# Decode attention in a hybrid encoder step: one sequence and four feature tiles at a time, instead of four sequences and one tile

## What is computed

```python
# fox: 8 heads of 64; diff: 4 heads, two maps of 64 each, values of 128
s = einsum('bqhd,bkhd->bhqk', q, concat(past_k, k)) * SCALE
s = s + cum[q] - cum[k]              # fox, and causal
s = s + bias[t5_bucket(k - q)]       # diff
p = softmax(s, axis=-1)
o = einsum('bhqk,bkhd->bqhd', p, concat(past_v, v))
# diff: a = p[map 0] - lam * p[map 1], then the same product
```

## Time and profile before

| | us |
|---|---|
| median of 3 runs | 2665.81 |
| lowest, highest | 2657.16, 2668.44 |
| profiled execution, its own time | 2663.46 |
| its span in the profile | 2661.7 |
| TensorE busy | 2517.9 (95%) |
| weight loads on TensorE busy | 2015.3 (76%) |
| VectorE busy | 1392.0 (52%) |
| ScalarE busy | 939.1 (35%) |
| GpSimd busy | 390.5 (15%) |
| granted TensorE clock, mean of the span | 0.978 |

### The profile page before, as it was taken

The page is one execution under the profiler, slowest core; times in us unless marked ns, Lnnn a source line. Parts: engine busy times, 40 slices in busy tenths (PEclk is TensorE's granted clock), DMA queues, the critical chain, the costliest instruction groups (busy, mean ns, idle before and its releaser), DMA issues.

```text
span 2661.7 us, 35813 instructions
## 1 busy us (share of the span) xinstructions
PE 2517.9 (95%) x13841; PEld 2015.3 (76%) x13841; DVE 1392.0 (52%) x2235; ACT 939.1 (35%) x1837; POOL 390.5 (15%) x398
## 2 busy tenths in 40 slices
PE   7999999998899999989989899899989989999998
PEld 5788888888799899989975565565556556888897
DVE  4311124413443333443248788788778876655553
ACT  4123331111122222100116655664664666422221
POOL 1100001131100000012244103213211340100000
PEclk9999999999899999999989999899999999999999
DMA  4543335448889889875842235055052322544432
GB/s 133 158 125 112 109 101 146 137 133 193 220 208 207 191 201 217 214 181 159 220 132 63 52 77 127 5 128 123 9 124 56 81 68 85 182 143 139 133 124 90
DMA packets 479945, 353.07 MB, mean 133 GB/s; under 512 B 189248, under 2 KB 443144, under 8 KB 473592
## 3 DMA queue, kind: packets, MB, share of 16 engines
q1 hardware_dynamic: 470640, 332.16, 48.8%
q0 software_dynamic: 9136, 18.63, 2.1%
HBM read 250.23 MB, written 100.19 MB: 132 GB/s over the span
## 4 chain that ended last, share of the span: by engine, by line
PE 73%; SPq 7%; DVE 6%; ACT 5%; issue 4%; DMA 4%; POOL 1%; DVEq 0%; ACTq 0%; POOLq 0%
PE p_acc L847 12%; PE p_acc L852 12%; PE p_acc L851 12%; PE a_op L2087 5%; PE a_sb L2062 4%; PE a_sb L2063 3%; PE a_op L2084 3%; SPq L467 3%; PE a_sa L2040 3%; PE a_sa L2043 2%; PE e_U L1404 2%; PE e_U L1405 2%; PE e_U L1406 2%; PE a_sa L2041 2%; ACT a_e L1900 2%
## 5 line engine op out<-in xcount | busy, mean ns | idle before, releaser
L847 PE MATMUL p_acc<-p_h_hi,p_w_hi 128*128 128x384 f32 (+1 forms) x1960 | 721.0, 368 | 9.4 <-DVE p_ev L559 8.0
L852 PE MATMUL p_acc<-p_h_hi,p_w_lo 128*128 128x384 f32 (+1 forms) x1920 | 689.2, 359 | 0.0
L851 PE MATMUL p_acc<-p_h_lo,p_w_hi 128*128 128x384 f32 (+1 forms) x1920 | 688.9, 359 | 0.0
L1931 DVE TENSOR_REDUCE a_nmax<-a_sa 128x1 f32<-128x1024 f32 (+7 forms) x384 | 347.2, 911 | 129.0 <-PE a_sa L2045 42.4
L1900 ACT ACTIVATE a_e<-a_sb 128x512 f32<-128x512 f32 (+3 forms) x640 | 310.4, 533 | 282.2 <-PE a_sb L2063 185.9
L847 PEld LDWEIGHTS p_acc<-p_h_hi,p_w_hi 128*128 128x128 f32 x1960 | 372.0, 190 | 48.2 <-DVE p_ev L559 8.3
L852 PEld LDWEIGHTS p_acc<-p_h_hi,p_w_lo 128*128 128x128 f32 x1920 | 362.9, 189 | 30.8
L851 PEld LDWEIGHTS p_acc<-p_h_lo,p_w_hi 128*128 128x128 f32 x1920 | 363.7, 189 | 28.7
L2062 PE MATMUL a_sb<-a_q,a_k 128*128 128x512 f32 (+2 forms) x640 | 277.3, 437 | 20.7 <-ACT a_e L1900 18.1
L661 DVE TENSOR_TENSOR p_w_lo<-p_raw,p_w_hi 128x1024 fp32r<-128x1024 f32 x96 | 129.5, 1349 | 304.5 <-ACT p_w_hi L592 304.5
L2063 PE MATMUL a_sb<-a_q,a_k 68*128 68x512 f32 (+2 forms) x640 | 237.9, 375 | 0.0
(11 more groups left out here) (228 smaller groups left out, 3569.4 us busy)
## 6 DMA issues: line engine op xcount, KB each, us to landing
p_raw<-in_w_in SPq DMA_DIRECT2D x98, 512.0 KB, 5.8
s_k_raw<-in_cache_fox_k SPq DMA_DIRECT2D x128, 128.0 KB, 3.8
s_v_raw<-in_cache_fox_v SPq DMA_DIRECT2D x32, 512.0 KB, 7.1
s_k_raw<-in_cache_diff_k SPq DMA_DIRECT2D x128, 128.0 KB, 3.9
s_v_raw<-in_cache_diff_v SPq DMA_DIRECT2D x32, 512.0 KB, 6.7
a_q<-scratch_q_hi SPq DMA_DIRECT2D x32, 512.0 KB, 13.3
a_k<-scratch_k_hi SPq DMA_DIRECT2D x32, 512.0 KB, 15.4
e_pair<-scratch_gT SPq DMA_DIRECT2D x80, 192.0 KB, 2.7
```

The lines of the kernel that those rows point to most:

```text
L847: nc.tensor.matmul(acc[a % 2][:, 0:n], hi, h_hi[p][:, k, at:at + n], start=(k == 0), stop=False)
L851: nc.tensor.matmul(acc[a % 2][:, 0:n], hi, h_lo[p][:, k, at:at + n], start=False, stop=False)
L852: last = nc.tensor.matmul(acc[a % 2][:, 0:n], lo, h_hi[p][:, k, at:at + n], start=False, stop=(k == DK - 1))
L1931: nc.vector.tensor_reduce(nmax[:, b % 2, c, col:col + 1], scores_of(ev[1]), axes, ALU.max, negate=True).then_inc(a_maxed, 1)
```

## The change

A unit now takes one sequence and four feature tiles, all fox or all diff: unit n is sequence n % 8 and tiles 0 to 3 (n < 8) or 4 to 7. Units 0 to 7 are still the fox ones, and the slots of all events are the same.

- A past key row is loaded whole, 2048 bytes, in 8 loads of 128 rows (L466 of the new file) instead of 16 loads in pieces of 256 bytes. Past values come in one load of 2 MB in pieces of 2048 bytes, instead of four of 512 KB in pieces of 512.
- Partitions 32i to 32i + 31 of the turned keys now hold the i-th quarter of the keys, for 32 of the features of every tile. The scores are 4 x 4 x 4 = 64 matmuls of 32 partitions by 32 columns with 256 keys, and 16 for the new keys. `tab` is four banks, a quarter of the keys in each, 272 columns (256 and room for the 16 new ones, filled with -1e30 in the first three).
- The small loads become 16 of q, 4 of new keys, and of `add` 16 for a fox unit (its 16 last columns apart) or 8 for a diff one.
- `turn` has two banks in place of three, for every user: `H`, `T`, `F` and `E`.
- The output store of a unit goes to four tiles, in pieces of 64 bytes.

```diff
-        k_raw = r_.sb("k_raw", [P, SEQS, 2 * KT, 2, 32])
-        v_raw = r_.sb("v_raw", [P, SEQS, KT, P])
-        kT = r_.sb("kT", [P, SEQS, 2, PAST // 2])
+        k_raw = r_.sb("k_raw", [P, KT, WIDTH])
+        v_raw = r_.sb("v_raw", [P, KT, WIDTH])
+        kT = r_.sb("kT", [P, KT, 4 * FTS, 32])
...
-        tab = s.ps("tab", [P, 3 * 512])
-        turn = [s.ps(f"turn{i}", [P, 512]) for i in range(3)]
+        tab = s.ps("tab", [P, 4, 512])
+        turn = [s.ps(f"turn{i}", [P, 512]) for i in range(2)]
...
-        return n // 2, n % 2, n // 2 >= 4
+        return n % DEC_BATCH, n // DEC_BATCH * FTS, n >= DEC_BATCH
...
-                for b in range(SEQS):
+                keys = cache("k", n).rearrange("(q t r) n -> t q r n", q=4, r=32)
+                for t in range(KT):
                     if n:
-                        sp.wait_ge(k_turned, 2 * (SEQS * (n - 1) + b + 1))
-                    for h in range(2):
-                        for m in range(2):
-                            at = 64 * h + 32 * m
-                            sp.dma_start(k_raw[at:at + 32, b], keys_of(n, b, h, m)).then_inc(k_in[b], 16)
+                        sp.wait_ge(k_turned, KT * (n - 1) + t + 1)
+                    sp.dma_start(k_raw[:, t], keys[t]).then_inc(k_in[t // 2], 16)
...
+                for j in range(4):
+                    rows_j = slice(32 * j, 32 * j + 32)
+                    for i in range(4):
+                        sp.dma_start(q_bd[32 * i:32 * i + 32, j, :, j // 2, :],
+                                     d["qT"][ft:ft + FTS, rows_j, tok].rearrange("f p t -> p f t")).then_inc(small_in, 16)
+                    sp.dma_start(kT_new[P - 32:P, j], d["kT"][ft:ft + FTS, rows_j, tok].rearrange("f p t -> p f t")).then_inc(small_in, 16)
...
+                            sp.dma_start(add[r:r + DEC_SEQ, :, 0:QK], d["nckS"][row:row + 1, 0:PAST].to_broadcast([DEC_SEQ, PAST])
+                                         .rearrange("p (q n) -> p q n", q=4)).then_inc(small_in, 16)
+                            sp.dma_start(add[r:r + DEC_SEQ, 3, QK:QW], d["nckS"][row:row + 1, PAST:KEYS]
+                                         .to_broadcast([DEC_SEQ, DEC_SEQ])).then_inc(small_in, 16)
...
-                for b in range(SEQS):
-                    sp.dma_start(v_raw[:, b], cache("v", n, b).rearrange("(t p) n -> p t n", p=P)).then_inc(v_in, 16)
+                sp.dma_start(v_raw[:], cache("v", n).rearrange("(t p) n -> p t n", p=P)).then_inc(v_in, 16)
...
             n = turn_at[ev_]
-            if n >= 3:
-                pe.wait_ge(turn_taken, n - 2)
-            return turn[n % 3]
+            if n >= 2:
+                pe.wait_ge(turn_taken, n - 1)
+            return turn[n % 2]
...
-                for j in range(2):
-                    for h in range(2):
-                        half = slice(64 * h, 64 * h + 64)
-                        for b in range(SEQS):
-                            q = q_bd[half, j, b].rearrange("p m t -> p (m t)")
-                            nc.tensor.matmul(tab[b * 32:b * 32 + 32, h * 512:h * 512 + 512], q, kT[half, b, j, :],
-                                             start=(j == 0), stop=(j == 1))
+                for j in range(4):
+                    for i in range(4):
+                        part = slice(32 * i, 32 * i + 32)
+                        for f in range(FTS):
+                            q = q_bd[part, j, f].rearrange("p m t -> p (m t)")
+                            nc.tensor.matmul(tab[f * 32:f * 32 + 32, i, 0:QK], q, kT[part, :, 4 * f + j, :],
+                                             start=(j == 0), stop=(j == 3))
```

More of the change, by code:

```diff
@@ L307, in project, with small_total, cache @@
     last_chunk = lambda g: (g, len(chunks(g)) - 1)
-    OP = 1152
+    scores = tab[:, :, 0:QW]
+    o_sum, o_turned = tab[:, 0, 288:288 + P], tab[:, 1, 288:288 + HD]
     PASS0 = max(acc_at[a] for a in acc_at if a[0] < NT) + 1
-    S_SMALL, S_V, S_K = 16 * 18, 16 * 5, 16 * 4
+    S_V, S_K = 16 * 2, 16 * 2
     def unit(n):
-        return n // 2, n % 2, n // 2 >= 4
-    def cache(name, n, b):
-        ft, g, diff = unit(n)
-        src = d[("cache_diff_" if diff else "cache_fox_") + name][0]
-        src = src.rearrange("b n h m e -> b n (h m e)" if diff and name == "k" else "b n h e -> b n (h e)")
-        return src[g * SEQS + b][:, ft % 4 * P:ft % 4 * P + P]
-    def keys_of(n, b, h, m):
-        half = cache("k", n, b)[h * 512:(h + 1) * 512, m * HD:(m + 1) * HD]
-        return half.rearrange("(t p) (j c) -> p t j c", p=32, c=32)
+        return n % DEC_BATCH, n // DEC_BATCH * FTS, n >= DEC_BATCH
+    def small_total(n):
+        return 16 * sum(20 + (8 if unit(i)[2] else 16) for i in range(n + 1))
+    def cache(name, n):
+        b, _, diff = unit(n)
+        src = d[("cache_diff_" if diff else "cache_fox_") + name][0]
+        return src.rearrange("b n h m e -> b n (h m e)" if diff and name == "k" else "b n h e -> b n (h e)")[b]
     def x_rows(t):
@@ L449, in sync @@
                 n = ev_[1]
-                ft, g, diff = unit(n)
+                b, ft, diff = unit(n)
                 if n == 0:
@@ L641, in scalar @@
                     act.wait_ge(v_inverted, n)
-                nc.scalar.activation(e_s[:], tab[:, 0:KEYS], ACT.Exp, bias=s_stat[:, 0:1], accum_out=s_stat[:, 1:2]).then_inc(weighed, 1)
+                nc.scalar.activation(e_s[:], scores, ACT.Exp, bias=s_stat[:, 0:1], accum_out=s_stat[:, 1:2]).then_inc(weighed, 1)
             elif what == "C1":
                 act.wait_ge(past_turned, 2)
-                nc.scalar.copy(line[:, 0:PAST], tab[0:BH, 0:PAST]).then_inc(line_made, 1)
+                nc.scalar.copy(line[:, 0:PAST].rearrange("p (h n) -> p h n", h=2), tab[0:BH, 0:2, :]).then_inc(line_made, 1)
     def vector(dve):
@@ L768, in vector @@
                 diff = unit(n)[2]
-                dve.wait_ge(small_in, S_SMALL * (n + 1))
+                dve.wait_ge(small_in, small_total(n))
                 if not diff:
-                    tail = add[:, PAST:KEYS]
+                    tail = add[:, 3, QK:QW]
                     nc.vector.tensor_tensor(tail, tail, causal, ALU.add).then_inc(added, 1)
@@ L774, in vector @@
                 dve.wait_ge(scored, n + 1)
-                cut = tab[:, PAST - P:KEYS] if diff else tab[:, 0:KEYS]
-                term = add[:, 0:P + DEC_SEQ] if diff else add[:]
+                cut = tab[:, 3, QW - P - DEC_SEQ:QW] if diff else scores
+                term = add[:, 3, QW - P - DEC_SEQ:QW] if diff else add[:]
                 nc.vector.tensor_tensor(cut, cut, term, ALU.add).then_inc(added, 1)
                 dve.wait_ge(added, n + 1 + min(n + 1, 8))
-                nc.vector.tensor_reduce(s_stat[:, 0:1], tab[:, 0:KEYS], AX.X, ALU.max, negate=True).then_inc(maxed, 1)
+                nc.vector.tensor_reduce(s_stat[:, 0:1], scores, AX.XY, ALU.max, negate=True).then_inc(maxed, 1)
             elif what == "E":
@@ L796, in vector @@
                     dve.wait_ge(merged, n)
-                nc.vector.tensor_scalar(o_rows[:], tab[:, OP:OP + P], s_stat[:, 2:3], coef[:, 6:7] if diff else coef[:, 7:8],
+                nc.vector.tensor_scalar(o_rows[:], o_sum, s_stat[:, 2:3], coef[:, 6:7] if diff else coef[:, 7:8],
                                         ALU.mult, ALU.mult).then_inc(rows_made, 1)
@@ L913, in tensor @@
                 for kt in range(KT + 1):
-                    for b in range(SEQS):
-                        v = v_raw[:, b, kt, :] if kt < KT else v_new[:, b, :]
-                        last = nc.tensor.matmul(tab[b * 32:b * 32 + 32, OP:OP + P], eT[:, kt, b * 32:b * 32 + 32], v,
+                    for f in range(FTS):
+                        v = (v_raw[:, kt] if kt < KT else v_new)[:, f * P:(f + 1) * P]
+                        last = nc.tensor.matmul(o_sum[f * 32:f * 32 + 32], eT[:, kt, f * 32:f * 32 + 32], v,
                                                 start=(kt == 0), stop=(kt == KT))
@@ L922, in tensor @@
                 if unit(n)[2]:
-                    last = nc.tensor.matmul(tab[:, OP + P:OP + P + HD], o_rows[:], sel[:, 2 * HD:3 * HD], start=True, stop=True)
+                    last = nc.tensor.matmul(o_turned, o_rows[:], sel[:, 2 * HD:3 * HD], start=True, stop=True)
                 else:
                     for m in range(2):
-                        last = nc.tensor.matmul(tab[m * HD:(m + 1) * HD, OP + P:OP + P + HD], o_rows[:, m * HD:(m + 1) * HD],
+                        last = nc.tensor.matmul(o_turned[m * HD:(m + 1) * HD], o_rows[:, m * HD:(m + 1) * HD],
                                                 sel[:, m * HD:(m + 1) * HD], start=True, stop=True)
```

115 lines of the change are left out of this document (57 added, 58 removed).

## The result

| | before | after |
|---|---|---|
| median, us | 2661.86 (4 runs) | 2857.93 (4 runs) |
| lowest, highest | 2657.16, 2668.44 | 2854.84, 2859.99 |
| span of the profiled execution | 2661.7 | 2854.6 |

The ratio is 1.0734, 95% interval 1.0704 to 1.0764: the change makes the kernel 196 us slower. The forecast was 2651, the range ended at 2690, and the dearest rival stood at 2689. The sign was that of R3, the size and the reason were nobody's.

A forecast was written before the change was run, and what follows sets the result against it. It took the 600 to 1240 us stage as TensorE-bound with 31.8 us of holes: 2663.5 - 19 (holes, clock) + 2.4 (scores) + 3 + 1.5 (turn banks) = 2651.4, forecast 2651; own range 2643 to 2658, overall low 2625, high 2690.

The forecast's parts named there:

- R3: Rival, scores on TensorE: a pass costs 28 ns whichever tile, decisive from 15 ns; slower, 2689 us; chance 0.18.
- Eight key loads of 128 pieces then cost 8 x 0.57 = 4.6 us.: SyncE's queue, per unit: key loads at an unhindered issue's price take 4.6 us instead of 12.1.
- A fox burst is then 4.6 + 8.6 + 7.3 = 20.5 us against 20.5 now: no gain.: SyncE's issue of one fox unit's keys, q with new keys, and add rows: 20.5 us, as long as before.
- "(b)" to "(e)": TensorE holes going: before o_rows, all 8.6 us; before unit 2's scores, 3.5; diff units, all 7.1; short ones, all 1.0.
- The value load, 0.6 us.: SyncE's queue: one value load costs 0.6 us if room counts pieces, gaining 6.4 us a unit; 7.0 if bytes.
- The packets under 512 bytes: Sign of being right: such DMA packets in the 600 to 1240 us stage fall from 165 thousand to about 65.
- Scores, +2.4 us.: TensorE's scores: past keys on sixteen tiles stay at 1.74 us, new keys add 0.15 us in 16 units.
- 10.6-fold for sixteen tiles: Alternative for TensorE's scores: half as long again, 2.6 us; stage pays 14 us more, forecast about 2665.
- Two turn banks, +3 and +1.5 us.: Turns waiting for DVE's copy of rows, 0.6 us in five units: +3 us; banks running out at the start: +1.5.
- The prediction's bound for a copy that waits for a store, 3 us: Two turn banks: if DVE's copy of rows itself waits for a store, up to 3 us in two of five units.
- The holes and clock: TensorE, 600 to 1240 us: 20.2 us of holes and 5 of slow clock go; three quarters kept, 19 us gained.
- new holes in the fox units behind the 36 small loads: Sign of being wrong: TensorE newly standing still in fox units behind their 36 small loads; no size given.

The follow-up runs named there:

- e1: The changed kernel with a unit's keys in 16 loads of 32 partitions by 2 runs of 2048 bytes instead of 8 loads: 2743.78 us, ratio to before 1.0307.
- e2: The changed kernel with a unit's keys in 16 loads, each with a source of 2 quarters by 32 rows: 3171.04 us in one run.
- e6: The kernel before with only the change's small loads (q 16, new keys 4, add 16 in a fox unit), each half as large: 2776.95 us, ratio 1.0411.
- e15: e5 with the edit of e14 (second-pass weights and stores of groups 0 to 39 issued by ACT): 2690.55 us, ratio 1.0098.
- e14: The kernel before with weights and stores of the second pass's groups 0 to 39 issued by ACT instead of SyncE: 2630.01 us, ratio 0.9862.
- e7: e5 with half of the score matmuls left out (two of the four blocks of 32 features): 2667.88 us in one run.
- e5: The changed kernel with a unit's keys in 4 loads and add in 5 loads for a fox unit, 4 for a diff one: 2706.02 us, ratio 1.0141.
- e8: The kernel of e1 with each score matmul of 256 keys cut into two of 128, the halves sixteen matmuls apart: 2819.87 us in one run.

## Why the prediction was wrong

*"Eight key loads of 128 pieces then cost 8 x 0.57 = 4.6 us."* This is the step that failed first. They cost 244 us in 16 units, 15.3 each. I took the price of an issue from the number of pieces, and the rate of the DMA engines (186 and 314 GB/s) from loads whose outermost dimension is 32 or 128. With 4 there, 4 engines carry the load (e1, e2). Undoing this alone (e1) gives 114 us back.

*"A fox burst is then 4.6 + 8.6 + 7.3 = 20.5 us against 20.5 now: no gain."* This is the second step that failed. It is 36.3. The rows of `add` are as predicted, 16 at 0.42 us. The q loads stand behind the keys and wait for them, 177 us in all against 110. And the idea behind the line, that 18 further issues are paid where a hole already is, is refuted by e6: they are paid in full, 111 us on the kernel before. The earlier trace rows showed the mechanism, and I counted six holes instead of adding up the queue. With 522 us of issues from 600 to 1240 beside a TensorE at 607, and weights and stores behind them, it had too little to spare. Measured alone, this mistake is as dear as the first, and the prediction's holes "(b)" to "(e)" hang on it: none went, and new ones of up to 23 us came beside them.

*The value load, 0.6 us.* Right: 0.43. Four times the bytes in as many pieces went out as fast as one of the four loads could, so room in the queue went by pieces here, and 80 us of issuing (87.0 to 7.1) went. The packets under 512 bytes fell to 62 thousand, 65 foretold. Both are true and neither helps when TensorE waits for the keys and the small loads.

*Scores, +2.4 us.* "Twice the tiles, half the time" was extended from eight tiles to sixteen, and does not hold there: 2.93 us a group, not 2.1, so 16 us at the full clock and 20 with the slow stretches. The past keys alone take 2.54 us (1058.03 to 1060.57), where the row-based sum had 1.74: 0.078 ns a column, where eight tiles had 0.106. The Trainium skill's 10.6-fold for sixteen tiles (TensorE: Matmul & The Clock Gate, Part 3, Measured speedup vs the span model), which the prediction set beside it, made 2.6 of it, and the trace agrees with that. R3's price of 28 ns a pass is refuted, a pass costs 14 to 19 ns; the 15 ns from which R3 was to decide were passed, but the passes did not decide.

*Two turn banks, +3 and +1.5 us.* 8.1 measured on the kernel before, 2.4 of it early. The prediction's bound for a copy that waits for a store, 3 us, was too low: 5.5 us more in one place.

*The chances.* The slower side had 0.18, all of it on the passes, which carry 20 of 196 us; that R3's sign came true is luck. The mechanism that decided, a queue near its limit made longer, stood in the text only as an argument for "no gain". The holes and clock went the way that the last paragraph named as proof of error, "new holes in the fox units behind the 36 small loads".

*What stays open.* The sums of the single effects do not add up to 196 (114 for the keys, 111 for the small loads, 60 for the new layout in e15 with its banks, less what the value load gives): they share one queue, and each was measured on another base. That the stops in mid-group are TensorE out of instructions rests on their spacing and on the packets before them, below, and was not tried by moving code; why those packets come late is open. Why a pass of 256 keys costs 18 ns on sixteen tiles was not separated from its weight load.

## What to carry to other kernels

Before a change adds issues to a queue, add up the time that the queue already spends issuing in that stage and compare it with the bound engine's: here it stood at 86% of it (522 of 607 us), and each added issue was paid in full. Then look at what stands behind those issues: in e14 the queue is as busy, and TensorE's holes are nearly gone, because nothing that the projections need waits behind the loads of a unit. Before a load is reshaped, look at the outermost dimension of both sides, not only at the length of the runs: 2048-byte runs on 4 engines moved 102 GB/s, where runs of 256 and 512 bytes on all of them moved 186 and 314. And what TensorE needs next is first of all to be taken out from behind long bursts: 0.986 came from sending two kinds of transfer through another engine's queue, without touching a single matmul, and only while the crowded stage lasted.

## What the runs showed of the hardware

*Few DMA engines look like a slow queue.* The issues of the key loads rose from 0.57 to 1.98 us in the median, as if the queue were slow. The sign was a DMA share of 0.26 while a queue was blocked.

*TensorE can run out of instructions.* The stops "<-issue" in the middle of a group or chunk, with no semaphore before them, come in the kernels whose scores are many short passes: 3.9 us in after, 23.6 us in e15, none in the second pass of the kernel before or of e7. A group in e5:

```profile
1082.35 2.76 PE L891 MATMUL p_tab<-s_kT,s_q_bd 32*32 32x256 f32 x128
1084.90 0.27 PE L896 MATMUL p_tab<-s_kT_new,s_q_bd 32*32 32x16 f32 x10
1088.17 0.51 PE L896 MATMUL p_tab<-s_kT_new,s_q_bd 32*32 32x16 f32 x22 [3.00 <-issue]
```

The packets of the instruction queue (packets, MB, share), on the pages of before, after and e8:

```profile
q8 instruction: 110, 1.80, 0.3%
```

```profile
q8 instruction: 124, 2.03, 0.3%
```

```profile
q8 instruction: 140, 2.29, 0.4%
```

A packet is 16 KB. After has 1792 matmuls and as many weight loads more than before (15633 against 13841), and 0.23 MB more of these packets: 64 bytes for each instruction. So a packet holds 256 instructions, 128 passes with their weight loads, and that is the spacing of the stops in e8. At 173 ns between the starts of a projection matmul such a packet lasts 22 us; in scores at 18 ns it lasts 2.3 us.

The packets' own times bear this out. In e5, e8 and e15 there are 36 stops of this kind of over 0.6 us, and each ends 2.3 to 3.1 us after the start of an instruction packet, which itself takes 0.9 to 1.6 us. The stop shown above ends at 1088.17; its packet starts at 1085.3, and there was none in the 16 us before. In the same three kernels the stops that stand before the first score of a unit, where the program waits, have their last packet 18 to 23 us back. Five of the stops come at the same matmul of the program in e1, e5 and e15, though at other times. What makes the packet start late, the data packets around it or something else, was not tested.
